# Modulation chunks of the first block taken quarter by quarter, with part of w_in between them

## What is computed

```python
mod = silu(c) @ w_ada + b_ada                       # 2048 x 12288
shift1, scale1, gate1, shift2, scale2, gate2 = split(mod, 6)
h = rms(x, norm1_w) * (1 + scale1) + shift1
u, q, k, v = split(h @ w_in, ...)                   # 2048 x 4096
y_ssm = s5_mixer(u, ...)                            # u is the "drive": first 1024 columns
y_att = dilated_attention(q, k, v, ...)
x = x + gate1 * (concat(y_ssm, y_att) @ w_out)
h2 = rms(x, norm2_w) * (1 + scale2) + shift2
x = x + gate2 * ((silu(h2 @ w_gate) * (h2 @ w_up)) @ w_down)
# second block: 16 meta tokens in front, FFN, pooling and attention mixer, FFN
```

## Time and profile before

| what | value |
|---|---|
| median of 3 executions | 3244.72 us (3244.39 to 3249.36) |
| profiled execution | 3248.48 us |
| its span on the core | 3246.7 us |
| PE busy | 3171.5 us (98%) |
| DVE busy | 1814.1 us (56%) |
| ACT busy | 1243.8 us (38%) |
| POOL busy | 157.0 us (5%) |
| mean granted PE clock | 0.979 |
| transferred | 631.92 MB |

### The profile page before, as it was taken

One profiled execution on the slowest core, in us unless ns is written; L12 is line 12 of the kernel. 1 busy time (PEld: TensorE's weight loads), 2 busy tenths in 40 slices (PEclk: granted clock), 3 DMA queues, 4 the chain that ended last, 5 costly groups with the idle time before them and its releaser, 6 DMA issues.

```text
span 3246.7 us, 56012 instructions
## 1 busy us (share of the span) xinstructions
PE 3171.5 (98%) x24596; PEld 3034.1 (93%) x24596; DVE 1814.1 (56%) x1689; ACT 1243.8 (38%) x1192; POOL 157.0 (5%) x182
## 2 busy tenths in 40 slices
PE   6799999999999999999999999999999999999999
PEld 3599979999999999999999999999999998998997
DVE  0699876776454545654444544555556544454454
ACT  2376634433333333433333333343334333333333
POOL 1434100000000000000000000000030000000000
PEclk7799999999999999999999999999999999999999
DMA  9876667776555555555555555566535555555554
GB/s 342 287 257 235 236 234 240 242 250 209 190 174 186 188 182 177 186 169 176 173 170 179 175 175 173 177 185 143 130 130 182 182 182 182 190 185 185 190 181 156
DMA packets 329090, 631.92 MB, mean 195 GB/s; under 512 B 22452, under 2 KB 24264, under 8 KB 328664
## 3 DMA queue, kind: packets, MB, share of 16 engines
q1 hardware_dynamic: 317896, 626.16, 59.4%
q10 hardware_dynamic: 11040, 3.51, 0.5%
HBM read 627.53 MB, written 2.10 MB: 194 GB/s over the span
## 4 chain that ended last, share of the span: by engine, by line
PE 81%; DVE 4%; issue 2%; ACT 1%; DMA 0%; DVEq 0%; ACTq 0%
PE ps L579 20%; PE ps L580 20%; PE ps L581 20%; PE ps L609 3%; PE ps L611 3%; PE ps L610 3%; PE ps L2037 2%; PE ps L2039 2%; PE ps L2038 2%; DVE w_lo L446 1%; ACT w_hi L441 1%; PE ps L2074 1%; PE ps L2076 1%; PE ps L2075 1%; PE ps L1811 1%
## 5 line engine op out<-in xcount | busy, mean ns | idle before, releaser
L446 DVE TENSOR_TENSOR w_lo<-raw,w_hi 128x2048 fp32r<-128x2048 f32 x496 | 1141.1, 2301 | 1218.1 <-ACT w_hi L441 1217.8
L441 ACT ACTIVATE w_hi<-raw 128x2048 fp32r<-128x2048 f32 x496 | 949.6, 1915 | 1676.2 <-PE ps L581 1291.3
L579 PE MATMUL ps<-act_hi,w_hi 128*128 128x258 f32 (+2 forms) x3328 | 953.9, 287 | 24.6 <-DVE w_lo L446 15.5
L580 PE MATMUL ps<-act_lo,w_hi 128*128 128x258 f32 (+2 forms) x3328 | 952.5, 286 | 0.0
L581 PE MATMUL ps<-act_hi,w_lo 128*128 128x258 f32 (+2 forms) x3328 | 950.5, 286 | 0.0
L579 PE MATMUL ps<-hid_hi,w_hi 128*128 128x256 f32 (+1 forms) x2816 | 796.0, 283 | 0.5 <-DVE w_lo L446 0.5
L580 PE MATMUL ps<-hid_lo,w_hi 128*128 128x256 f32 (+1 forms) x2816 | 795.5, 282 | 0.0
L581 PE MATMUL ps<-hid_hi,w_lo 128*128 128x256 f32 (+1 forms) x2816 | 794.3, 282 | 0.0
L579 PEld LDWEIGHTS ps<-act_hi,w_hi 128*128 128x128 f32 x3328 | 631.8, 190 | 29.1 <-issue 15.0
L580 PEld LDWEIGHTS ps<-act_lo,w_hi 128*128 128x128 f32 x3328 | 631.7, 190 | 0.1
L581 PEld LDWEIGHTS ps<-act_hi,w_lo 128*128 128x128 f32 x3328 | 631.3, 190 | 0.0
(11 more groups left out here) (371 smaller groups left out, 2810.1 us busy)
## 6 DMA issues: line engine op xcount, KB each, us to landing
raw<-in_w_ada SPq DMA_DIRECT2D x96, 1024.0 KB, 6.0
raw<-in_ffn_w_gate SPq DMA_DIRECT2D x88, 1024.0 KB, 5.2
raw<-in_ffn_w_up SPq DMA_DIRECT2D x88, 1024.0 KB, 5.1
raw<-in_ffn_w_down SPq DMA_DIRECT2D x88, 1024.0 KB, 5.1
raw<-in_w_in SPq DMA_DIRECT2D x64, 1024.0 KB, 6.6
raw<-in_w_ffn_gate SPq DMA_DIRECT2D x44, 1024.0 KB, 5.1
raw<-in_w_ffn_up SPq DMA_DIRECT2D x44, 1024.0 KB, 5.2
raw<-in_w_ffn_down SPq DMA_DIRECT2D x44, 1024.0 KB, 5.1
```

The costliest lines, as they stand in the source:

```text
L441: act.activation(w_hi[b][:, :, :], raw[j % RING][:, :, :], ACT.Copy).then_inc(hi_ready, 1)
L446: dve.tensor_tensor(w_lo[b][:, :, :], raw[j % RING][:, :, :], w_hi[b][:, :, :].bitcast(F32), ALU.subtract).then_inc(lo_ready, 1)
L579: pe.matmul(o, whi, hi_, start=(k == 0 and not (shared and m % 2)), stop=False)
L580: pe.matmul(o, whi, lo_, start=False, stop=False)
```

## The change

1. `ada1` becomes one iteration with the order `VVVVVVVVSS` four times. A quarter of it is one column group of scale1, the same group of shift1, and then two S chunks: the rows of `w_in` for these 512 features, for the two column groups of the drive.
2. PE does strips, gathers and the products of the drive (`first_in`) in between; DVE and ACT do the bias, gain and norm of one quarter and the splits of its two chunks before the next.
3. The rest of `w_in` is one iteration of 24 S and 32 V chunks with the order `SVSVSVV` eight times. The state-space turns get a table `SLOT_AT` instead of the rule; other tables (`HEADS_AT`, `GATE1_AT`) shift with it. The drive's rows are moved out by `drive_out` after the eighth and ninth S chunk's splits.
4. The loads of the mixer's parameters on ACT come behind the first quarter and its products on PE move to the second to fourth; some buffers lie elsewhere.
5. The order of `ffn1.up0` goes from `SSVSSVSSVSSV` to `SSSSVSVSSVSV`.

```diff
-            add(f"{name}.up{i}", groups, 2, 4, "SSVSSVSSVSSV" if name == "ffn1" and i == 0 else None)
+            add(f"{name}.up{i}", groups, 2, 4, "SSSSVSVSSVSV" if name == "ffn1" and i == 0 else None)
-    add("ada1", 8, 0, 4, "VVVV")
-    add("w_in", 4, 2, 4, "SV" * 8)
+    add("ada1", 1, 2, 4, "VVVVVVVVSS" * 4)
+    add("w_in", 1, 6, 4, "SVSVSVV" * 8)
...
+        def drive_out(act, g):
+
+            act.wait_ge(chunk_done, 7 + g)
+            src = half_tiles(g)
+            for t in range(4):
+                for j in range(STEP):
+                    ins = act.activation(proj[32 * j:32 * j + 32, 4 * g:4 * g + 4, step_cols(t)],
+                                         src[32 * t:32 * t + 32, :, j:SEQ:STEP], ACT.Copy)
+            ins.then_inc(bank_free[g], 2)
...
-        BASE = 5
+        SLOT_AT = (8, 9, 10, 11, 12, 13, 14, 15, 16, 17, 18, 19, 19, 20, 21, 22, 23, 24, 24, 25, 26, 27, 28, 29, 29, 30, 31)
...
+                for q in range(QUADS):
+                    split_hi(act, ada, 0, 10 * q + 8)
+                    norm_act(act, q)
+                    split_hi(act, ada, 0, 10 * q + 9)
...
+                for q in range(QUADS):
+                    if q:
+                        strip_copy(2 * q)
+                    strip_copy(2 * q + 1)
+                    dve.wait_ge(mod_sum, 2 * q + 2)
...
+                    norm_dve(dve, q, lambda: split_lo(dve, ada, 0, 10 * q + 8))
+                    split_lo(dve, ada, 0, 10 * q + 9)
...
+                strips(0, range(4))
+                square_sums()
+                pe.wait_ge(res_in, QUADS + 1)
+                strips(1, range(4))
+                group_sum(0)
+                group_sum(1)
+                for q in range(1, QUADS):
+                    first_in(2 * q - 2)
+                    strips(2 * q, (0, 1))
+                    first_in(2 * q - 1)
+                    strips(2 * q, (2, 3))
+                    if q == 1:
                         params_pe(pe)
+                    else:
+                        c_turns(2 * q - 4)
+                    strips(2 * q + 1, (0,))
+                    group_sum(2 * q)
+                    if q > 1:
+                        c_turns(2 * q - 3)
+                    strips(2 * q + 1, (1, 2, 3))
+                    group_sum(2 * q + 1)
+                first_in(6)
+                first_in(7)
```

More of the change, by code:

```diff
@@ L470, in acc_of, with run_phase @@
             return buf[:, it, :] if isinstance(it, int) else buf[:, bass.ds(it, 1), :].rearrange("p a n -> p (a n)")
-        def run_phase(eng, name, split, evac, pending, acc=None, norm=False, ahead=None, peel=1, beside=None):
+        def run_phase(eng, name, split, evac, pending, acc=None, ahead=None, peel=1, beside=None):
             p = byname[name]
@@ L659, in root_dve, with norm_dve @@
             link(dve, "dve", dve.reciprocal(rstd[:, :], rstd[:, :]))
[L661 to L680, removed]
+        def norm_dve(dve, q, second):
+            v = (val, sig)[q % 2]
+            if q >= 2:
+                dve.wait_ge(act_ready, ACT0["norm1"] + q - 1)
+            for k in range(4 * q, 4 * q + 4):
+                dve.scalar_tensor_tensor(out=v[:, k % 4, :], in0=res[:, k, :], scalar=gain[:, k:k + 1],
+                                         in1=rstd[:, :], op0=ALU.mult, op1=ALU.mult).then_inc(norm_val, 1)
+            second()
+            for k in range(4 * q, 4 * q + 4):
+                dve.wait_ge(norm_val, k + 1)
+                dve.wait_ge(norm_bias, k + 1)
+                ins = dve.scalar_tensor_tensor(out=act_lo[:, k, :], in0=v[:, k % 4, :], scalar=mod[:, SHIFT1 + k:SHIFT1 + k + 1],
+                                               in1=act_hi[:, k, :].bitcast(F32), op0=ALU.add, op1=ALU.subtract)
+            ins.then_inc(act_ready, 1)
         ACT0 = {}
@@ L762, in step_cols, with half_tiles @@
             return slice(META + STEPS * t, META + STEPS * t + STEPS)
+        def half_tiles(half):
+            return ps[:, 2 * half:2 * half + 2, :].rearrange("p b (q n) -> p (b q) n", q=2)
+        def drive_out(act, g):
[6 more added lines that the diff above has]
+            ins.then_inc(bank_free[g], 2)
         def copy_out(act, p, it, g):
             group_done(act, p, it, g)
[L767 to L777, removed]
+            src = half_tiles(g % 2)
+            k = 8 + 4 * g
             if k == 24:
@@ L1500, in _ @@
-                act.wait_ge(c_turned, 1)
-                for r in range(2):
-                    for h in range(2):
[L1503 to L1507, removed]
-                flush = run_phase(act, "w_in", split_hi, bind(act, copy_out), lambda: norm_act(act, "norm1", 0), peel=4,
-                                  beside=lambda m: (sums_act(act, m), ssm_act(act, m), heads_act(act, m)))
+                root_act(act, "norm1")
@@ L1568, in _, with square_sums @@
                 mm.then_inc(x_t, 1)
-                def square_sums(qs):
-                    for q in qs:
+                def square_sums():
+                    for q in range(QUADS):
                         pe.wait_ge(sq_ready, q + 1)
@@ L1606, in _, with c_turns @@
-                pe.wait_ge(acc_copied, 8)
-                gather(pe, acc1[:, 7, :], 5, 28)
-                products(pe, "w_in", act_hi, act_lo, SEQ_COLS, counted(act_ready, ACT0["norm1"]), beside=lambda m: ssm_pe(pe, m))
+                def c_turns(b):
+                    r, half = divmod(b, 2)
+                    if b == 0:
+                        pe.wait_ge(pre_act, 8)
+                    for i in range(4):
+                        mm = pe.transpose(ps[:, 6 + b % 2, P * i:P * i + P], cd[:, 8 * r + 4 * half + i, :, :].rearrange("p d n -> p (d n)"), ident)
+                    mm.then_inc(c_turned, 1)
@@ new lines, in _, with strips @@
+                ada = byname["ada1"]
+                def strips(g, js):
+                    q, part = divmod(g, 2)
+                    for j in js:
+                        if j == 0 and g >= 2:
+                            pe.wait_ge(acc_copied, g - 1)
+                        if j == 0 and g >= 5:
+                            pe.wait_ge(*((c_read, g - 4) if g < 8 else (c_ready, 1)))
+                        n = 10 * q + 4 * part + j
+                        landed(pe, ada, 0, n)
+                        for t in range(CK):
+                            pe.matmul(ps[32 * t:32 * t + 32, 7 - g % 2, :], cond32[:, CK * j + t, :], raw[n % RING][:, t, :],
+                                      start=(j == 0), stop=(j == 3)).then_inc(acc_step, 1)
@@ L1609, in _ @@
+                first_in(6)
+                first_in(7)
+                pe.wait_ge(c_ready, 1)
+                products(pe, "w_in", act_hi, act_lo, SEQ_COLS, counted(act_ready, ACT0["norm1"]), beside=lambda m: ssm_pe(pe, m + 8))
                 pe.wait_ge(y_ready, BLOCKS)
```

185 lines of the change are left out of this document (104 added, 81 removed).

## The result

The changed kernel takes 3261.49 us (median of 5 executions, 3257.2 to 3262.89) against 3244.51 us before: a ratio of 1.0048, with a 95% interval of 1.0036 to 1.006. It is slower by 17 us in these medians, where about 5 less were forecast. Its profiled execution took 3257.2 us with a span of 3255.4; that of before took 3248.48. The two traces thus lie 8.7 us apart, the medians 17: single executions of one kernel spread over some 5 to 13 us in these runs (13 us in 30 executions of the kernel before), so the traces serve to find the place and the medians to weigh it.

The account below looks back on a forecast made before the run. Transfers bound the head; PE and DVE are both full from 160 to 352 us. A 14.4 us gain in `ffn1.up0` and a loss of 9 in `w_in` sum to about −5: 3240 us, range 3229 to 3253.

Parts of the forecast that it names:

- The head: Before the rest of `w_in`: first drive product at 49.3 us, quarters of 34.5, last quarter's products at 153.6 (148 to 158).
- The start of the rest of `w_in`: First split 9.9 us behind the products at 153.6; then 6.3 us of waits behind the drive's copies on ACT.
- DVE's remaining work: Rest of `w_in`: 235.4 us of work left for DVE, all 32 V chunks among them, ending at 405.2.
- the one on the moved loads and tables: Parameter loads, turned matrices and tables: nothing, or under 1 us each quarter if their products ran into its end.
- the loss put down for the quarters: Head and `w_in`: next stage at 409 us against 399.87, a loss of 9 us (4 to 15).
- The tail: End of `w_in`: head norms and five small operations in 1.2 us, then 2.8 until PE's next stage, at 409.
- The reorder: `ffn1.up0`: waits at three boundaries shrink from 2.95 to 0.2 us; gain 14.4, or 8.3 if only idle time goes.
- The slower one: Rival in the rest of `w_in`: paired V chunks starve PE, its clock falls; 5 to 20 us, middle 3250; chance 0.16.
- The faster one: Rival in the head: transfers set the pace, quarters of 31 us or less, `w_in` breaks even; 3230; chance 0.18.
- The reorder did what it says: Against the rival in `ffn1.up0` that the reorder does not: gain 0 to 8 us, time about 3250; chance 0.09.
- GpSimd did not hold DVE up: Against the rival that GpSimd does in the second quarter: products start 10 us later, 3249; chance 0.05.

Follow-up runs that it names:

- sums-ahead: Changed kernel with the small sums of doubled turns (m = 19, 24, 29) put ahead of the same turn's state products: 3242.97 us, ratio 0.9995.
- the quarters alone: Changed kernel with the old order of `ffn1.up0`: 3270.79 us, ratio 1.0077.
- later gathers: Kernel with the small sums ahead, first three gathers of gate1 at m = 14, 17, 19 instead of 11, 14, 17: 3242.96 us, ratio 0.9996.
- the narrow chunks: Kernel with the small sums ahead, every fourth V chunk of `w_in` multiplied on 32 of 512 columns only: 3235.51 us, ratio 0.9976.
- the strips ahead: Changed kernel with each quarter's first two strips ahead of the first drive product, the next two ahead of the second: 3255.37 us, ratio 1.0037.

## Why the prediction was wrong

**The head: right.** First product at 49.21 (49.3 was forecast), quarters of 34.2 on average (34.5), the last one's products at 151.8 (153.6), PE idle 6.4 us behind each chain on DVE (6.5). The Trainium skill ("DMA: Bandwidth & Descriptors", section "Anatomy of one DMA — SWDGE (gpsimd) path") would have made quarters of 33.5 by an estimate from that page; the measured 33.4 to 35.5 lie around both and don't tell them apart.

**The start of the rest of `w_in`: right.** First split at 161.79, that is 10.0 behind the products (9.9), then idle times of 1.88, 3.75 and 0.69 behind the drive's copies, 6.3 together (6.3). The drive's copies cost what was put down for them.

**DVE's remaining work: right.** From 161.79 to 413.17 are 251.4 us; without 19.2 idle that leaves 232.2 (235.4).

**The step that failed** is the one on the moved loads and tables. It named the tables and priced them, with the buffers, at nothing. `SLOT_AT` was the table with a price. Twenty-seven turns had to go on 24 S chunks, three chunks got two, and in those a hand-over from PE to ACT and back lost the product that had covered it. The price is 18.5 us in the medians, by taking it away. What it needed was in the kernel's text: `small_sums` waits for `y_ready` at the head of a block's first turn, and two equal numbers in the table put this right behind the products that `y_ready` waits for. The duration was in the trace of before too, 4.65 us for the copy. The sum with it would have been −14.4 + 9 + 3 x 4.65 = +8.5, if nothing covers the three waits.

One more premise goes with this. The prediction gave PE 3 us of slack in each cycle of 29.3 us, which would have hidden much of such waits. In the sums-ahead trace PE idles 4.0 of the 90 us from 200 to 290, where three cycles would give 9, at a clock of 0.94; so there was little slack to hide them in. In the changed kernel 12.7 us of idle time on DVE follow the three waits (5.16, 1.51 and 5.99).

With the doubled turns mended, the loss put down for the quarters, 9, is what the medians show: the sums-ahead kernel is 9.4 us slower than the reorder alone (3242.97 against 3233.58). That it fits so well is in part luck. In the sums-ahead trace DVE's last V chunk ends at 400.9, 4.3 us before the forecast, and the stage begins 6.5 behind it, not 4. Of the 21.5 us between forecast and result, 18.5 are thus the doubled turns and 3 the reorder, which gave 11.4 instead of 14.4.

**The tail: wrong, for the most part as a consequence.** 4 us between DVE's end and the next stage were forecast and 9.3 measured, since PE, not DVE, was last (its products end at 418.7). Without the doubled turns it is 6.5.

**The reorder: right in kind, its size between the bounds.** The wait is 0.2 us, as forecast. An iteration takes 46.5 us where 46.0 was forecast, so the traces give 12.9 us; the medians give 11.4 alone and 9.3 with the quarters. All lie between the bounds of 8.3 and 14.4, and the forecast took the upper one, from an execution that was itself 3.8 us over its median. What a boundary costs with the old order differs from one to the next: in the trace of the quarters alone the iterations take 51.9 and 49.3 us. How often the clock falls there in other executions stays open, since each kernel has one profiled execution.

**The rivals.** The slower one had the right sign and a mechanism of a like kind (PE waits and its clock falls), at the wrong place: later gathers moved its waits for nothing, and the narrow chunks gave back 5 us. The faster one fell: quarters stayed above 33, and even with the strips ahead they reached 29 to 33. The reorder did what it says. GpSimd did not hold DVE up: with GpSimd at work beside it, DVE's chain from the bias to the end of `act_lo` takes 6.4 us in the second quarter (78.3 to 84.7) and 6.3 in the third, where 0.8 more was put down and 10 feared. The 2 us more that this quarter took come ahead of that chain, at the late chunks and the gather.

## What to carry to other kernels

A table that spreads n turns over fewer places puts two of them into one, and what stood between them was a cover: look up each pair for a wait of the second on what the first one started on another engine, and price it with the duration of that engine's work. Where two full engines both lose busy time after a change, as here, the cause may lie with neither; look in the list of waits for a third. Then ask whom a wait is for. PE's waits for DVE could be moved at no gain, as the later gathers show, since DVE was the bound and was late anyway. PE's waits for ACT cost their full length, since PE, held up by them, came to hold up DVE.

The fastest version of these runs is the kernel before with the new order of `ffn1.up0` alone, 3233.58 us.

## What the runs showed that was not expected

Three waits of PE, an engine with idle time in this stage, cost at least their own length: 14.3 us of waits, 15.1 at the next stage, 18.5 in the medians. Behind each, PE ran at half its clock: the stretch from 260 to 290 us shows a granted clock of 0.83, and the 16 small sums took 3.57 instead of 1.93 us. How much of the price is the clock's is not shown. The head shows the same from the other side: with products between the strips PE's clock still falls once per quarter, behind each idle piece of 6.4 us, and each first product begins at 0.4 to 0.6 us per instruction where later ones take 0.28.
